# Hybrid streaming encoder step: forget rows spread by DMA, sample values with the probabilities stationary in four column groups, two attention phases one chunk earlier

## The chip, the cores and the metric

One core of one Trainium2 chip runs the kernel. The metric is the time on the device in microseconds (us), the median of several runs. All data are 32-bit floats.

## The reference, cut to what matters

Two layers work on 256 prompt frames and 32 sample frames (288 columns). Each layer is norm, one input projection, two kinds of attention of 8 heads each, output projection, residual, then norm and a squared-ReLU MLP. Phases A (sparse top-k) and B (forgetting) belong to layer 0, C (stick-breaking) and D (chunk band) to layer 1. The sample frames also see 512 cached keys. What the change touches:

```python
# B, forgetting attention; cum is the inclusive sum of log-forget values
logits = einsum('bthd,bshd->bhts', q, k) * scale
logits = logits + swapaxes(cum_q, 1, 2)[..., None] - cum_k   # one row per head, the same for all queries
probs = softmax(where(k_pos <= q_pos, logits, NEG_INF))
out = einsum('bhts,bshd->bthd', probs, v)
# C: the same last step with stick-breaking weights; D: logits + rel_bias, visible band only
```

## The kernel before

**The weight stream.** All weights come in 756 chunks of 128 x 1024 over SP's queue. ACT copies each to `w_high` (L784), DVE subtracts to get `w_low` (L1063), and TensorE multiplies high*high, high*low and low*high (L352 to L354, and L318 to L320 in the output projections), 24 matmuls of 288 columns a chunk.

**Attention beside it.** Each phase has 10 jobs: eight prompt heads (n = 0 to 7, `n < H`) and two sample jobs (n = 8, 9), each of four heads with 32 queries. Phase A runs beside the chunks of B's input projection, B beside the first half of the output projection (`out_half(..., 0, ...)`, 16 chunks), C beside D's input projection, D beside the second layer's first output half. After chunk w every engine does its "window w": the steps that `START[ph][n]` and `jobs_at(ph, w, late)` give. A job's scores come in window START, its turn (transposes of the probabilities) one later, its values two later for prompt jobs, three (C: four) for sample jobs; on ACT and DVE the exponentials (`before`) and `normalize` precede the chunk's work of the next window, and the order inside a window is fixed by hand. After half 0 the second half starts, which waits for the last `mixed_low` of its phase.

**Names.** `logits` adds bias and mask and takes the maximum; `mixed_high` and `mixed_low` (L903, L1272) copy a result of `values` into the projection's operands. `norm_sums` (L434), `rsqrt` (L842, L845) and `prelude` (L1210) normalise pairs of heads: pairs 4 to 7 are the queries, in windows 0 and 1 of B and D, from POOL's `squares` (L1586). `early` does D's first pairs from window 34 of C on. POOL also loads the biases (L1601), adds the mask (`masked`, L1614) and loads the cached keys and values (L1589, L1592). B's forget rows `neg_cum` are added by matmuls of 8 rows (the second pair at L509 and L510, and L490). Sample values are L560 and L562.

Of the kernel before, what the change touches and what calls it, by code (L numbers as in the profile page):

```python
# [14 lines left out]
P = 128  # L15
D = 2048
# [65 lines left out]
WINDOWS = {ph: s[-1] + (5 if ph == "C" else 4) for ph, s in START.items()}  # L82
# [49 lines left out]
def build(nc, ins, outs):  # L132
    with ExitStack() as ctx:
# [49 lines left out]
        neg_cum = sb("neg_cum", [H, TP + L])  # L183
# [23 lines left out]
        def pair_squares(ph, i):  # L207
            return sqs_dq[i % 2] if ph == "D" and i >= 4 else sqs[i % 2]
# [42 lines left out]
        small = proj[0:SMALL, 16, :]  # L251

# [44 lines left out]
        def _(pe):  # L297
# [176 lines left out]
            def scores(ph, n):  # L474
                c = PH[ph]
                if n == 0:

                    pe.wait_ge(sem(ph + "_normed"), (8 + c["nkv"]) // 2)
                    if ph == "A":
                        pe.wait_ge(sem("B_cum_copied"), 1)  # L480
                if n < H:
# [4 lines left out]
                    for (at, keys), queries in zip(HALVES, (q[:, P:TP], q[:, 0:P])):  # L486
                        last = pe.matmul(ps[:, b, at:at + keys], queries, k[:, 0:keys], start=True, stop=ph != "B")  # L487
                        if ph == "B":

                            last = pe.matmul(ps[:, b, at:at + keys], ident[0:H, n:n + 1].to_broadcast([H, P]),  # L490
                                             neg_cum[:, 0:keys], start=False, stop=True)
                else:
                    u = n - H
                    pe.wait_ge(sem(ph + "_s_read"), n)
                    if ph == "A" and n == H:

                        pe.wait_ge(sem("B_rsqrt"), 4)
                    pe.wait_ge(sem(ph + "_k_past"), 16 * (u + 1) if ph != "A" else 16)
                    for j in range(4):
                        h = 4 * u + j  # L500
                        q = q_tiles(ph, h)[:, 0, TP:T]
                        kp, kn = (k_past[ph][:, u, :], u) if ph == "A" else (k_past[ph][:, j, :], h)
                        pairs_ = [(q, kp, k_tile(ph, kn)[:, TP:T])]
                        if ph == "B":
                            pairs_.append((ident[0:H, h:h + 1].to_broadcast([H, TS]), neg_cum[:, TP:TP + PAST],
                                           neg_cum[:, TP + PAST:TP + L]))
                        for m, (lhs, past, new) in enumerate(pairs_):
                            flags = dict(start=m == 0, stop=m == len(pairs_) - 1)
                            pe.matmul(flat[32 * j:32 * j + 32, 2048:2048 + PAST], lhs, past, **flags)  # L509
                            last = pe.matmul(flat[32 * j:32 * j + 32, 2048 + PAST:2048 + L], lhs, new, **flags)  # L510
                last.then_inc(sem(ph + "_scored"), 1)

            def turn_rest(ph, n):

                pe.wait_ge(sem(ph + "_pt_copied"), H + 2 * (n - H) + 1)
                pe.transpose(ps[0:TS, 6, 0:P], probs[n % 2][:, PAST:L], ident[:, :]).then_inc(sem(ph + "_turned"), 1)

            def turn(ph, n):

                pe.wait_ge(sem(ph + "_probs"), n + 1)  # L520
                if n >= 1:
                    pe.wait_ge(sem(ph + "_pt_copied"), n if n <= H else n + (n - H))
# [5 lines left out]
                else:  # L528
                    for b in range(4):
                        last = pe.transpose(ps[:, 6, b * P:b * P + P], p[:, b * P:b * P + P], ident[:, :])  # L530
                    last.then_inc(sem(ph + "_turned"), 1)

            def values(ph, n):
# [5 lines left out]
                else:  # L539
                    pe.wait_ge(sem(ph + "_pt_copied"), n + 1 if n < H else H + 2 * (n - H + 1))  # L540
# [6 lines left out]
                else:  # L547
# [105 lines left out]
            def window_c(w):  # L653
                prelude("C", w)
                for n in jobs_at("C", w, 3, 4):
# [118 lines left out]
        def _(act):  # L774
# [102 lines left out]
            def pt_copy(ph, n):  # L877
                w = pt[n % 2]
                if n >= 2:

                    act.wait_ge(sem(ph + "_mixed"), n - 1)
                if n < H:
                    act.wait_ge(sem(ph + "_turned"), n + 1)
                    act.activation(w[:, 0:384], ps[:, 6, 0:384], ACT.Copy).then_inc(sem(ph + "_pt_copied"), 1)
                else:
                    act.wait_ge(sem(ph + "_turned"), H + 2 * (n - H) + 1)
                    act.activation(w[:, 0:512], ps[:, 6, 0:512], ACT.Copy).then_inc(sem(ph + "_pt_copied"), 1)

            def pt_copy_rest(ph, n):
                act.wait_ge(sem(ph + "_turned"), H + 2 * (n - H) + 2)  # L890
# [947 lines left out]
```

## Time and profile before

| | |
|---|---|
| median of 3 runs | 2680.01 us (2679.99 to 2680.86) |
| the profiled execution | 2679.78 us, of which the span of the profile is 2678.0 us |
| mean granted TensorE clock | 0.986 of full |
| TensorE matmuls busy | 2639.0 us (99%) |
| VectorE / ScalarE / GpSimd busy | 54% / 37% / 6% |

In a timeline a row is start, duration, engine, line, operation, output<-inputs, rows*columns of the stationary operand, and its count; consecutive matmuls overlap, so the cost of one is the distance to the next start. An fp32 matmul leaves two records. In a windows table a row is the stretch and its length, then the busy us and instructions of PE, PEld, DVE, ACT and POOL (of PE alone where only that was asked for), the granted clock, the DMA share and GB/s. A clock of 1.00 is 2.4 GHz, 0.50 is 1.2 GHz.

### The profile page before, as it was taken

What the parts mean: (1) busy time and instruction counts of PE and PEld (TensorE: products, weight loads), DVE (VectorE), ACT (ScalarE), POOL (GpSimd) and SP (SyncE); (2) the same over time, 40 slices, a digit from 0 to 9 for tenths busy, and PEclk for the clock granted to TensorE, in tenths of its full rate; (3) what the DMA queues carried; (4) which work ended last, traced back from release to release, by engine and by line L of the source; (5) the groups of instructions that cost most, each with busy time, mean ns of one, the idle gap of its engine ahead of it and who ended that gap; (6) DMA issues with size and microseconds to landing.
All of it is one profiled execution on the core that took longest, in us unless ns stands there. A gap on an engine that the chain in (4) does not pass through costs nothing.

```text
span 2678.0 us, 47174 instructions
## 1 busy us (share of the span) xinstructions
PE 2639.0 (99%) x19365; PEld 2580.8 (96%) x19365; DVE 1443.2 (54%) x1630; ACT 996.6 (37%) x1233; POOL 173.2 (6%) x162
## 2 busy tenths in 40 slices
PE   7999999999999999999999999999999999999998
PEld 7989987999999999999999999999999999999998
DVE  6577753754455455455654553558544544544543
ACT  4443442433333333333333442434333333333332
POOL 2011110300000000000200001213000000000000
PEclk9999998999999999999999998999999999999999
DMA  5535432445444555554455543534454555554453
GB/s 204 173 131 166 153 125 95 142 166 165 166 167 166 166 167 167 166 167 164 160 200 166 177 152 131 170 138 158 166 166 165 167 166 167 166 168 167 166 179 132
DMA packets 116350, 431.35 MB, mean 161 GB/s; under 512 B 13936, under 2 KB 14272, under 8 KB 113856
## 3 DMA queue, kind: packets, MB, share of 16 engines
q1 hardware_dynamic: 109440, 398.77, 44.8%
q0 software_dynamic: 5664, 29.56, 3.1%
q8 instruction: 152, 2.49, 0.4%
q10 hardware_dynamic: 1056, 0.22, 0.0%
q14 instruction: 38, 0.31, 0.0%
HBM read 418.31 MB, written 10.11 MB: 160 GB/s over the span
## 4 chain that ended last, share of the span: by engine, by line
PE 96%; DVE 1%; issue 1%; ACT 1%; DMA 0%; SPq 0%; POOL 0%; DVEq 0%; ACTq 0%; POOLq 0%
PE ps L352 27%; PE ps L354 27%; PE ps L353 27%; PE ps L318 3%; PE ps L319 3%; PE ps L320 3%; PE ps L560 1%; PE ps L434 1%; PE ps L509 1%; PE ps L545 1%; PE ps L487 1%; DVE w_low L1063 0%; ACT w_high L784 0%; PE ps L722 0%; PE ps L562 0%
## 5 line engine op out<-in xcount | busy, mean ns | idle before, releaser
L1063 DVE TENSOR_TENSOR w_low<-raw,w_high 128x1024 fp32r<-128x1024 f32 x756 | 952.4, 1260 | 962.7 <-ACT w_high L784 960.1
L784 ACT CAST w_high<-raw 128x1024 fp32r<-128x1024 f32 x756 | 793.3, 1049 | 1472.8 <-PE ps L354 1359.5
L352 PE MATMUL ps<-x_parts,w_high 128*128 128x288 f32 x3472 | 1041.0, 300 | 18.5 <-DVE x_parts L1132 14.5
L353 PE MATMUL ps<-x_parts,w_high 128*128 128x288 f32 x3472 | 1025.1, 295 | 0.0
L354 PE MATMUL ps<-x_parts,w_low 128*128 128x288 f32 x3472 | 1023.4, 295 | 0.0
L352 PEld LDWEIGHTS ps<-x_parts,w_high 128*128 128x128 f32 x3472 | 653.8, 188 | 25.0 <-issue 16.0
L353 PEld LDWEIGHTS ps<-x_parts,w_high 128*128 128x128 f32 x3472 | 659.0, 190 | 3.0 <-issue 2.4
L354 PEld LDWEIGHTS ps<-x_parts,w_low 128*128 128x128 f32 x3472 | 657.9, 189 | 0.0
L352 PE MATMUL ps<-hid_parts_a,w_high 128*128 128x288 f32 x1024 | 303.1, 296 | 0.0
L354 PE MATMUL ps<-hid_high_b,w_low 128*128 128x288 f32 x1024 | 302.3, 295 | 0.0
L353 PE MATMUL ps<-hid_low_b,w_high 128*128 128x288 f32 x1024 | 302.3, 295 | 0.0
L352 PE MATMUL ps<-hid_high_b,w_high 128*128 128x288 f32 x1024 | 301.5, 294 | 0.0
L353 PE MATMUL ps<-hid_parts_a,w_high 128*128 128x288 f32 x1024 | 301.2, 294 | 0.0
L354 PE MATMUL ps<-hid_parts_a,w_low 128*128 128x288 f32 x1024 | 300.8, 294 | 0.0
L353 PEld LDWEIGHTS ps<-hid_parts_a,w_high 128*128 128x128 f32 x1024 | 193.5, 189 | 0.0
L352 PEld LDWEIGHTS ps<-hid_parts_a,w_high 128*128 128x128 f32 x1024 | 191.9, 187 | 1.5 <-DVE w_low L1063 1.5
L354 PEld LDWEIGHTS ps<-hid_parts_a,w_low 128*128 128x128 f32 x1024 | 193.3, 189 | 0.0
L353 PEld LDWEIGHTS ps<-hid_low_b,w_high 128*128 128x128 f32 x1024 | 192.4, 188 | 0.0
L354 PEld LDWEIGHTS ps<-hid_high_b,w_low 128*128 128x128 f32 x1024 | 192.3, 188 | 0.0
L352 PEld LDWEIGHTS ps<-hid_high_b,w_high 128*128 128x128 f32 x1024 | 192.1, 188 | 0.0
L318 PE MATMUL ps<-hid_parts_a,w_high 128*128 128x288 f32 x256 | 82.0, 320 | 0.7 <-DVE hid_parts_a L1272 0.7
L318 PE MATMUL ps<-hid_high_b,w_high 128*128 128x288 f32 x256 | 79.4, 310 | 1.4 <-DVE hid_low_b L1272 1.4
(316 smaller groups left out, 1986.5 us busy)
## 6 DMA issues: line engine op xcount, KB each, us to landing
raw<-in_w SPq DMA_DIRECT2D x756, 512.0 KB, 3.3
resid<-in_x SPq DMA_DIRECT2D x4, 576.0 KB, 7.4
out_y<-resid POOLq DMA_DIRECT2D x8, 288.0 KB, 2.4
scr<-in_k_past_B POOLq DMA_DIRECT2D x2, 1024.0 KB, 5.2
scr<-in_v_past_B POOLq DMA_DIRECT2D x2, 1024.0 KB, 6.1
scr<-in_k_past_C POOLq DMA_DIRECT2D x2, 1024.0 KB, 6.7
scr<-in_v_past_C POOLq DMA_DIRECT2D x2, 1024.0 KB, 8.4
scr<-in_k_past_D POOLq DMA_DIRECT2D x2, 1024.0 KB, 5.9
```

The costliest lines, as they stand in the source:

```text
L318: pe.matmul(out, wh, high, start=k % 8 == 0, stop=False)
L319: pe.matmul(out, wh, low, start=False, stop=False)
L320: last = pe.matmul(out, w_low[:, c % 2, at:at + P], high, start=False, stop=k % 8 == 7)
L352: pe.matmul(out, wh, high, start=k == 0, stop=end and apart)
L353: pe.matmul(out_low, wh, low, start=k == 0 and apart, stop=False)
L354: last = pe.matmul(out_low, w_low[:, kk % 2, at:at + rows], high, start=False, stop=end)
L434: last = pe.matmul(ps[:, b + u, 0:T], ones[:, :], pair_squares(ph, i)[:, u, :], start=True, stop=True)
L487: last = pe.matmul(ps[:, b, at:at + keys], queries, k[:, 0:keys], start=True, stop=ph != "B")
L509: pe.matmul(flat[32 * j:32 * j + 32, 2048:2048 + PAST], lhs, past, **flags)
L545: pe.matmul(ps[:, 7, 0:TP], v[:, 0, :], w[:, 0:TP], start=True, stop=False)
L784: act.copy(w_high[:, kk % 2, :], raw[:, kk, :]).then_inc(high_ready, 1)
L1063: dve.tensor_tensor(w_low[:, kk % 2, :], raw[:, kk, :], w_high[:, kk % 2, :].bitcast(F32), ALU.subtract)\
```

## The change

Four things are edited. (1) `neg_cum` is written once to a DRAM tensor `cum_rows`, and for each B job a DMA spreads its row over the partitions of `addend`; POOL adds the mask and DVE takes `addend` in place of the mask, so that the 8-row matmuls go. (2) Sample values of B, C and D use the probabilities (128 x 32) as stationary and the values (128 columns) as moving operand, each head in its own group of 32 output partitions; ACT copies the rows out (`copy_rows`, in B and D with the division by the sum) and one transpose (`turn_mixed`) a window later brings them back. (3) Jobs of B and D start one window earlier, the last job of A too, and C's sample outputs come one window later. (4) The transposes of a sample job are in one window, and POOL orders bias, mask and squares anew (`addends_beside`).

```diff
 START = {
-    "A": [23 + n for n in range(H)] + [43, 46],
-    "B": [2 + n for n in range(H)] + [10, 12],
+    "A": [23 + n for n in range(H)] + [43, 45],
+    "B": [1 + n for n in range(H)] + [9, 11],
     "C": [1 + 3 * n for n in range(H)] + [25, 29],
-    "D": [2 + n for n in range(H)] + [10, 12],
+    "D": [1 + n for n in range(H)] + [9, 11],
 }
...
-WINDOWS = {ph: s[-1] + (5 if ph == "C" else 4) for ph, s in START.items()}
+WINDOWS = {ph: s[-1] + (6 if ph == "C" else 3 if ph == "A" else 4) for ph, s in START.items()}
...
-        neg_cum = sb("neg_cum", [H, TP + L])
+        neg_cum = sb("neg_cum", [H, WIDE + L])
+        cum_rows = nc.dram_tensor("cum_rows", (H, WIDE + L), F32).ap()
...
-            return sqs_dq[i % 2] if ph == "D" and i >= 4 else sqs[i % 2]
+            return sqs_dq[i % 2] if ph in "BD" and i >= 4 else sqs[i % 2]
...
+        def rows_out(ph, n):
+
+            return (xs if ph == "C" else probs)[n % 2][:, 0:HD]
+
+        def mixed_at(ph, n):
+
+            return ps[:, 7, P:2 * P] if n >= H and ph != "A" else ps[:, 7, 0:P]
...
+                if n == 0 and ph == "A":
+                    pe.wait_ge(sem("A_normed"), (8 + c["nkv"]) // 2)
+                    pe.wait_ge(sem("B_cum_copied"), 1)
+                if ph in "BD" and n < H:
+                    pe.wait_ge(sem(ph + "_normed"), 4 + n // 2 + 1)
+                    if n == 0:
+                        pe.wait_ge(sem(ph + "_ln"), 7)
+                    if n == 1:
+                        pe.wait_ge(sem(ph + "_ln"), 8)
...
-                        last = pe.matmul(ps[:, b, at:at + keys], queries, k[:, 0:keys], start=True, stop=ph != "B")
-                        if ph == "B":
-
-                            last = pe.matmul(ps[:, b, at:at + keys], ident[0:H, n:n + 1].to_broadcast([H, P]),
-                                             neg_cum[:, 0:keys], start=False, stop=True)
+                        last = pe.matmul(ps[:, b, at:at + keys], queries, k[:, 0:keys], start=True, stop=True)
...
+                    if u:
+                        pe.wait_ge(sem(ph + "_pt_copied"), n)
...
-                        pairs_ = [(q, kp, k_tile(ph, kn)[:, TP:T])]
-                        if ph == "B":
-                            pairs_.append((ident[0:H, h:h + 1].to_broadcast([H, TS]), neg_cum[:, TP:TP + PAST],
-                                           neg_cum[:, TP + PAST:TP + L]))
-                        for m, (lhs, past, new) in enumerate(pairs_):
-                            flags = dict(start=m == 0, stop=m == len(pairs_) - 1)
-                            pe.matmul(flat[32 * j:32 * j + 32, 2048:2048 + PAST], lhs, past, **flags)
-                            last = pe.matmul(flat[32 * j:32 * j + 32, 2048 + PAST:2048 + L], lhs, new, **flags)
+                        pe.matmul(flat[32 * j:32 * j + 32, 2048:2048 + PAST], q, kp, start=True, stop=True)
+                        last = pe.matmul(flat[32 * j:32 * j + 32, 2048 + PAST:2048 + L], q, k_tile(ph, kn)[:, TP:T],
+                                         start=True, stop=True)
...
-            def turn_rest(ph, n):
-
-                pe.wait_ge(sem(ph + "_pt_copied"), H + 2 * (n - H) + 1)
-                pe.transpose(ps[0:TS, 6, 0:P], probs[n % 2][:, PAST:L], ident[:, :]).then_inc(sem(ph + "_turned"), 1)
...
-                pe.wait_ge(sem(ph + "_probs"), n + 1)
+                pe.wait_ge(sem(ph + ("_probs" if n < H or ph == "A" else "_exps")), n + 1)
...
-                        last = pe.transpose(ps[:, 6, b * P:b * P + P], p[:, b * P:b * P + P], ident[:, :])
-                    last.then_inc(sem(ph + "_turned"), 1)
+                        pe.transpose(ps[:, 6, b * P:b * P + P], p[:, b * P:b * P + P], ident[:, :])
+                    pe.transpose(ps[0:TS, 5, 384:512], p[:, PAST:L], ident[:, :]).then_inc(sem(ph + "_turned"), 1)
...
+                        for b in range(4):
+                            for j in range(4):
+                                at = b * P + TS * j
+                                pe.matmul(ps[TS * j:TS * j + TS, 7, 0:HD], w[:, at:at + TS], v_past[ph][:, b, j, :],
+                                          start=b == 0, stop=False)
                         for j in range(4):
-                            out = ps[:, 7, TS * j:TS * j + TS]
-                            for b in range(4):
-                                pe.matmul(out, v_past[ph][:, b, j, :], w[:, b * P + TS * j:b * P + TS * j + TS],
-                                          start=b == 0, stop=False)
-                            last = pe.matmul(out, v_new[ph][0:TS, 2, 4 * u + j, :],
-                                             w[0:TS, PAST + TS * j:PAST + TS * j + TS], start=False, stop=True)
+                            at = PAST + TS * j
+                            last = pe.matmul(ps[TS * j:TS * j + TS, 7, 0:HD], w[0:TS, at:at + TS],
+                                             v_new[ph][0:TS, 2, 4 * u + j, :], start=False, stop=True)
...
+            def turn_mixed(ph, n):
+
+                pe.wait_ge(sem(ph + "_rows_copied"), n - H + 1)
+                pe.transpose(mixed_at(ph, n), rows_out(ph, n), ident[:, :]).then_inc(sem(ph + "_rows_turned"), 1)
...
-                for n in jobs_at(ph, w, 2, 3):
+                for n in jobs_at(ph, w, 3):
+                    if n >= H and ph in "BD":
+                        turn_mixed(ph, n)
+                for n in jobs_at(ph, w, 2):
                     values(ph, n)
...
-                for n in jobs_at(ph, w, 2):
-                    if n >= H:
-                        turn_rest(ph, n)
...
+                for n in jobs_at("C", w, 5):
+                    if n >= H:
+                        turn_mixed("C", n)
...
+                act.wait_ge(sem(ph + "_mixed"), n + 1)
+                if ph == "C":
+                    act.activation(rows_out(ph, n), ps[:, 7, 0:HD], ACT.Copy).then_inc(sem(ph + "_rows_copied"), 1)
+                else:
+                    act.wait_ge(sem(ph + "_inv"), n - H + 1)
+                    act.activation(rows_out(ph, n), ps[:, 7, 0:HD], ACT.Copy, scale=inv[:, n % 2, 0:1])\
+                       .then_inc(sem(ph + "_rows_copied"), 1)
...
+                for n in jobs_at("C", w, 3, 5):
                     mixed_high("C", n)
+                for n in jobs_at("C", w, 4):
+                    if n >= H:
+                        copy_rows("C", n)
...
+                if n < 2 and ph in "BD":
+                    dve.wait_ge(sem(ph + "_normed"), 7 + n)
                 if ph == "B":
-                    if n == 0:
-                        dve.wait_ge(sem("B_masks"), 32)
+                    dve.wait_ge(sem("B_addend"), n + 1)
...
-                                mask_b[:, at:at + keys], ALU.add, ALU.add)
+                                addend[n % 2][:, at:at + keys], ALU.add, ALU.add)
...
+                if n >= H and ph in "BD":
+                    dve.reciprocal(inv[:, r, 0:1], total[:, r, 0:1]).then_inc(sem(ph + "_inv"), 1)
+                    return
...
+                landed_ = sem(f"{ph}_bias{n % 2}")
+                if ph == "B":
+
+                    pool.wait_ge(sem("B_rows"), 16)
+                    if n < H:
+                        pool.dma_start(addend[n % 2][:, 0:WIDE], cum_rows[n:n + 1, 0:WIDE].to_broadcast([P, WIDE]))\
+                            .then_inc(landed_, 16)
+                    else:
+                        for j in range(4):
+                            h = 4 * (n - H) + j
+                            pool.dma_start(addend[n % 2][TS * j:TS * j + TS, 0:L],
+                                           cum_rows[h:h + 1, WIDE:WIDE + L].to_broadcast([TS, L])).then_inc(landed_, 16)
+                    return
...
+                elif ph == "B":
+                    if n == 0:
+                        pool.wait_ge(sem("B_masks"), 32)
+                    m = mask_b if n < H else mask_bs
...
+                    if n == 0:
+                        pool.wait_ge(sem("D_mask"), 16)
...
+            def addends_beside(ph):
+
+                for n in range(2):
+                    masked(ph, n)
+                squares(ph, 4, 8)
+                for n in range(2, JOBS):
+                    bias(ph, n)
+                    if n - 1 >= 2 and (n - 1 < H or ph == "B"):
+                        masked(ph, n - 1)
+                if ph == "B":
+                    masked(ph, JOBS - 1)
...
+            pool.wait_ge(sem("B_cum_copied"), 1)
+            pool.dma_start(cum_rows[:, :], neg_cum[:, :]).then_inc(sem("B_rows"), 16)
...
-            squares("B", 4, 6)
+            bias("B", 0)
+            bias("B", 1)
             pool.wait_ge(hid_low_ready, hid_at["B"])
             load_quad("B", 0)
             load_quad_v("B", 0)
-            squares("B", 6, 8)
+            addends_beside("B")
             second_quad("B")
...
-            squares("D", 4, 8)
-            pool.wait_ge(sem("D_mask"), 16)
-            addends("D", 0, JOBS)
+            bias("D", 0)
+            bias("D", 1)
+            addends_beside("D")
```

## Rows read from the trace of the kernel before

**Rows 1.** The page: busy time by engine, and the chain that ended last, by engine.
```profile
PE 2639.0 (99%) x19365; PEld 2580.8 (96%) x19365; DVE 1443.2 (54%) x1630; ACT 996.6 (37%) x1233; POOL 173.2 (6%) x162
...
PE 96%; DVE 1%; issue 1%; ACT 1%; DMA 0%; SPq 0%; POOL 0%; DVEq 0%; ACTq 0%; POOLq 0%
```

**Rows 2.** Windows table: chunks alone; first of seven half-clock stretches, their sum.
```profile
560.00:700.00 140.00, 140.00 (x1060) 140.00 (x1059) 70.47 (x68) 50.25 (x50) 0.00 (x0) 1.00 0.50 166
...
345.71:355.84 10.13, 9.08 (x36) 8.27 (x36) 0.63 (x2) 0.55 (x2) 1.12 (x2) 0.50 0.58 208
...
sum 60.19, PE 58.14 PEld 55.95 DVE 4.53 ACT 5.18 POOL 5.59; mean PE 8.31 PEld 7.99 DVE 0.65 ACT 0.74 POOL 0.80
```

**Rows 3.** Windows table of TensorE alone: six single jobs, start to end.
```profile
415.93:424.20 8.27, 8.27 (x33) 1.00 0.19 65
1765.57:1766.64 1.07, 1.07 (x17) 1.00 0.10 32
366.06:368.04 1.98, 1.98 (x11) 1.00 0.13 52
1725.38:1726.01 0.63, 0.63 (x6) 1.00 0.47 189
336.92:338.31 1.39, 1.39 (x12) 1.00 0.65 165
1794.08:1799.41 5.33, 5.33 (x42) 1.00 0.57 189
```

**Rows 4.** Timeline of TensorE: sample scores of B (one head), then D's.
```profile
415.93 1.05 PE L509 MATMUL ps<-scr,proj 128*32 128x512 f32 x2
...
416.97 1.04 PE L509 MATMUL ps<-neg_cum,ident 8*32 8x512 f32 x2
...
1765.57 1.08 PE L509 MATMUL ps<-scr,proj 128*32 128x512 f32 x8
```

**Rows 5.** Timeline of TensorE: tail of A and its last waits, then B's.
```profile
344.31 0.66 PE L530 MATMUL ps<-ident,tmp 128*128 128x128 f32 x4 [1.47 <-DVE tmp L1259]
345.71 0.40 PE L516 MATMUL ps<-ident,tmp 128*32 128x128 f32 x1 [0.75 <-ACT scr L887]
...
349.96 0.61 PE L318 MATMUL ps<-hid_parts_a,w_high 128*128 128x288 f32 x1 [0.69 <-DVE hid_parts_a L1272]
...
466.88 0.61 PE L318 MATMUL ps<-hid_high_b,w_high 128*128 128x288 f32 x1 [0.69 <-DVE hid_low_b L1272]
```

**Rows 6.** Timeline of DVE and POOL around A's end.
```profile
342.14 2.11 DVE L1259 TENSOR_SCALAR tmp<-tmp,inv 128x544 f32<-128x544 f32 x1
...
341.69 2.26 POOL L1586 TENSOR_TENSOR acc<-proj 128x576 f32<-128x576 f32 x2
350.20 0.58 POOL L1589 DMA_DIRECT2D scr<-in_k_past_B  x1 [6.26 <-DVE hid_parts_a L1272]
```

**Rows 7.** Timeline of ACT, DVE, POOL: C's last window but one, and D's first loads.
```profile
1652.92 1.04 ACT L784 CAST w_high<-raw 128x1024 fp32r<-128x1024 f32 x1 [1.76 <-PE ps L354]
...
1654.00 1.23 DVE L1063 TENSOR_TENSOR w_low<-raw,w_high 128x1024 fp32r<-128x1024 f32 x1 [2.51 <-ACT w_high L784]
1659.64 0.29 DVE L1272 TENSOR_TENSOR hid_parts_a<-ps,hid_parts_a 128x128 fp32r<-128x128 f32 x1 [4.41 <-ACT hid_parts_a L903]
...
1660.22 0.55 POOL L1690 DMA_DIRECT2D scr<-in_mask_d  x1 [32.96 <-DVE hid_parts_a L1272]
```

**Rows 8.** Timeline of DVE and TensorE: D's last query pair, first logits, first turn.
```profile
1724.32 0.96 DVE L1210 SCALAR_TENSOR_TENSOR proj<-proj,qk_gain,tmp 128x576 f32<-128x576 f32 x1 [0.53 <-ACT tmp L845]
...
1727.86 0.55 DVE L1236 TENSOR_TENSOR tmp<-ps,acc 128x384 f32<-128x384 f32 x1
...
1730.92 0.33 PE L525 MATMUL ps<-ident,tmp 128*128 128x128 f32 x1 [1.50 <-DVE tmp L1256]
```

**Rows 9.** The page: DMA issues, KB each, median us from issue to landing.
```profile
scr<-in_k_past_B POOLq DMA_DIRECT2D x2, 1024.0 KB, 5.2
...
acc<-in_bias_A POOLq DMA_DIRECT2D x8, 192.0 KB, 3.5
```

More of the change, by code:

```diff
@@ L902, in mixed_high, with copy_rows @@
                     f = f0 + 4 * (n - H)
-                    act.activation(hid(True, f, 4)[:, :, TP:T], ps[:, 7, 0:P].rearrange("p (j t) -> p j t", j=4),
+                    act.activation(hid(True, f, 4)[:, :, TP:T], mixed_at(ph, n).rearrange("p (j t) -> p j t", j=4),
                                    ACT.Copy).then_inc(hid_high_ready, 1)
+            def copy_rows(ph, n):
+                act.wait_ge(sem(ph + "_mixed"), n + 1)
+                if ph == "C":
[4 more added lines that the diff above has]
+                       .then_inc(sem(ph + "_rows_copied"), 1)
             def attend(ph, w):
+                for n in jobs_at(ph, w, 3):
+                    if n >= H and ph in "BD":
+                        mixed_high(ph, n)
                 for n in jobs_at(ph, w, 1):
@@ L909, in attend @@
                 for n in jobs_at(ph, w, 2):
-                    if n >= H:
-                        pt_copy_rest(ph, n)
-                for n in jobs_at(ph, w, 2, 3):
-                    mixed_high(ph, n)
+                    if n >= H and ph in "BD":
+                        copy_rows(ph, n)
+                    else:
+                        mixed_high(ph, n)
             def dots_relu(x):
@@ L1225, in logits @@
                                 p[:, at:at + keys], ps[:, 4 + n % 2, at:at + keys], cum_q[:, 1 - i, n:n + 1],
[L1226 removed]
+                                addend[n % 2][:, at:at + keys], ALU.add, ALU.add)
                     else:
                         last = dve.scalar_tensor_tensor(p[:, 0:L], flat[:, 2048:2048 + L],
[L1229 removed]
+                                                        cum_qs[:, n - H:n - H + 1], addend[n % 2][:, 0:L],
+                                                        ALU.add, ALU.add)
                 else:
@@ L1252, in normalize @@
                 m = 2 if n < H else 1
+                if n >= H and ph in "BD":
+                    dve.reciprocal(inv[:, r, 0:1], total[:, r, 0:1]).then_inc(sem(ph + "_inv"), 1)
+                    return
                 link(dve.reciprocal(inv[:, r, 0:m], total[:, r, 0:m]))
@@ L1277, in attend @@
                     logits(ph, n)
-                for n in jobs_at(ph, w, 2, 3):
+                for n in jobs_at(ph, w, 2, 3 if ph in "BD" else 2):
                     mixed_low(ph, n)
@@ L1462, in window_c @@
                     scale_q()
-                for n in jobs_at("C", w, 3, 4):
+                for n in jobs_at("C", w, 3, 5):
                     mixed_low("C", n)
@@ L1598, in bias @@
                     pool.wait_ge(sem(ph + "_s_read"), n - 1)
+                landed_ = sem(f"{ph}_bias{n % 2}")
[4 more added lines that the diff above has]
+                            .then_inc(landed_, 16)
+                    else:
+                        for j in range(4):
[3 more added lines that the diff above has]
+                    return
                 a, rows = (addend[n % 2][:, 0:WIDE], ins["bias_" + ph][n]) if n < H else \
                     (addend[n % 2][:, 0:L], ins[f"bias_{ph}_s"][n - H])
-                pool.dma_start(a, rows).then_inc(sem(f"{ph}_bias{n % 2}"), 16)
+                pool.dma_start(a, rows).then_inc(landed_, 16)
             def masked(ph, n):
-                pool.wait_ge(sem(f"{ph}_bias{n % 2}"), 16 * (n // 2 + 1))
+                pool.wait_ge(sem(f"{ph}_bias{n % 2}"), 16 * (n // 2 + 1) + (48 if ph == "B" and n >= H else 0))
                 a = addend[n % 2][:, 0:WIDE] if n < H else addend[n % 2][:, 0:L]
```

29 lines of the change are left out of this document (11 added, 18 removed).

## The prediction

> **What bounds the kernel.** I read the page first: TensorE has matmuls in flight 99% of the time, and the chain that ended last runs through it for 96% [rows 1]. So the time is TensorE's work, and the question is what each of its jobs costs from start to start, not how long a record is. Next the windows table, for the clock. A chunk is 24 x 140 / 1060 = 3.17 us at full clock, 3.3 behind fp32 matmuls [rows 2]. In seven stretches of together 60.19 us the granted clock is at half, 1.2 GHz; TensorE is busy in 58.14 us of them [rows 2]. One opens in the waits at A's tail, two in or behind sample values of B, two of C, two of D; ahead of six of them TensorE ran small matmuls of 32 moving columns. Then single jobs in the timeline [rows 3, 4], and last the ends and beginnings of phases, where TensorE does wait [rows 5 to 8].
>
> **Forget rows.** A sample job's scores in B take 8.27 us, in D, where there are no forget rows, 1.07 us, although the rows themselves are only half of B's matmuls [rows 3]. The timeline says why: D issues the matmuls of its four heads, each in its own 32 output partitions, as one group of 8 records in 1.08 us; B's first head alone takes 1.04 us from its start to that of its 8-row matmul [rows 4]. The alternation of 128-row and 8-row operands keeps the four groups apart. Without it B's job should be D's: 2 x (8.27 - 1.07) = 14.4 us. A prompt job's scores: 1.98 us against D's 0.63, 8 x 1.35 = 10.8 us. Together 25.2 us. On the other side stand DMAs that I price at nothing: a row spread over 128 partitions is 192 KB, as A's bias, which lands in 3.5 us [rows 9]; jobs follow each other by (1765.57 - 1725.38) / 8 = 5.0 us in D [rows 3] and each buffer has two of these. DVE's sum has as many inputs as before, and POOL's ten mask additions lie beside chunks.
>
> **Sample values.** One job at full clock takes 5.33 us for 20 matmuls [rows 3]. The new job has as many, of 128 moving columns. The nearest row for that shape is A's: five in 1.39 us [rows 3], four in a column of 128 cached keys and one of 32 rows. The change gives each of four heads exactly five, in four column groups. If the groups run side by side as D's scores do, the job costs about 1.4 us; if they don't, 4 x 1.39 = 5.6. I take 1.4, because D's four heads cost what B's one does. Six jobs: 6 x (5.33 - 1.4) = 23.6 us. The six added transposes come at some 0.2 us each (bounds 0.1 and 0.4; four in a row take 0.66 us to the end of the last [rows 5]), 1.2 us back: 22.4 us. ACT's row copies are hidden by a whole chunk, as the transpose comes one window later.
>
> The Trainium skill (TensorE: Matmul & The Clock Gate, Part 3, what overlaps and what doesn't) says that a weight load overlaps with matmuls in flight only when its row group differs. In the new job all cached keys fill all rows and each matmul has its own weights, so by that rule the groups would queue and the job would be nearer 5.6 us. D's scores, which also load weights in between, ran side by side in 1.07 us, so the trace speaks against it; the row has long matmuls, though, and these are short.
>
> **The clock.** The low stretches begin with the jobs that become short, so I take them all as gone: half of 58.14 is 29.1 us. That includes C's second sample job, whose 32-column scores stand right behind the values and ran at half speed. The bounds are no gain at all, if each fall finds another cause, and all 29.1.
>
> **Ends of phases.** A's last job moves from window 46 to 45, so its values no longer lie behind the last chunk with nothing beside. In place of waits of 1.47, 0.75 and 0.69 us [rows 5], I expect 0.2 at the turn (DVE's multiplication took 2.11 us while POOL squared [rows 6]; the squares now come later) and 1.3 before the output half: behind the last chunk ACT's cast, DVE's subtraction and then `mixed_low` stand in line, 2.7 us after the chunk, against 1.4 of values. Saved: 2.91 - 1.5 = 1.4 us. At the ends of B and D the last job is complete a window before half 1, so 0.69 us each is saved [rows 5], D as B. Together 2.8 us.
>
> **New waits.** They come from the earlier start and from a faster TensorE.
> - B, window 0: `squares` 4 and 5 were done by 344 [rows 6]. Now they stand behind two key and value loads (released 0.25 us after the half begins, 1.1 us) and two mask additions (each 1.1, as the squares' 1.13), and squares 4 itself takes 1.13: ready after 4.7 us, while TensorE arrives after one chunk, 3.3 us. Wait 1.4, and 0.35 for the second: 1.75 us.
> - First job of D: the scores come right behind the last `norm_sums` and wait 0.25 us for ACT's read of the bank. The logits must wait for both query pairs, 1724.32 + 0.96 = 1725.28. From logits to turn the chain is 1730.92 - 1727.86 = 3.06 us [rows 8], so the turn is at 1728.4, while TensorE, which before came to its first scores at 1725.38 [rows 3], arrives there plus 0.63 and 0.25, at 1726.2: 2.2 us. That is 2.45 against 1.50 before: 0.95 us. In B the same 2.45 against a wait of 0.27 before: 2.2 us.
> - From C to D: `early` D still begins in window 34, and `turn_mixed` of C's last job is now in that window too. Its copy waits on ACT behind the cast, its `mixed_low` on DVE behind the subtraction: in window 33 the cast begins at 1652.92, an estimated 0.25 us behind its chunk, and the subtraction ends at 1655.23 [rows 7], so 2.6 us after the chunk, then 0.29. POOL follows 0.29 later [rows 7], issues three DMAs (1.63 us) and squares (1.13): 5.9 us, of which 0.3 is the transpose. Wait 5.6 us. Before, values and a chunk at half speed covered all of it. Such a gap is longer than those at A's tail behind which the clock fell, so I add a half-clock stretch of some 6 us, 3.0 us.
> - Second key loads of B wait for POOL's last mask addition. Between the two sample jobs lie two chunks and their jobs, some 8 us, and a load needs 0.6 + 5.2 [rows 6, 9]. I take nothing, up to 2 us.
>
> Together 1.75 + 0.95 + 2.2 + 5.6 + 3.0 = 13.5 us.
>
> **The sum.** - 25.2 - 22.4 - 29.1 - 2.8 + 13.5 = - 66.0 us. The profiled execution took 2679.78 us, 1.78 more than its span and 0.2 under the median, so both give 2613.8, I say 2614 us.
>
> **Rivals.**
> - The column groups queue (chance 0.09; the skill's rule above): 6 x 4.2 = 25 us less gain, 2639 us. For it: 32-wide weights are loaded 40 times a job. Against: D's scores.
> - The clock falls elsewhere (0.16): at the waits at B's and D's start, and at C's second sample scores, which keep their 32-column matmuls. Three stretches of the common 6.8 us give 10 us back, 2624 us. For it: TensorE is idle 2 us at a time there. Against: before D's 1.50 us no fall followed.
> - The gap from C to D is short, or the clock stands it (0.10): up to 8.6 us better, 2605 us.
> - Slower than before (0.02): the spread rows land late, since 128 partitions read one DRAM row. Two job periods less POOL's and DVE's part, some 7 us, are free; beyond that each job waits half the excess, and with ten jobs a landing of 20 us would eat all 66. A's bias needs 3.5, so this needs nearly six times as much.
> - No effect within 0.2% (0.01): only if several of these fall together.
> - My forecast (0.62): 2608 to 2620 us.
>
> The likeliest is 2614. The range reaches down to the short gap and a share of the tails, 2603, and up past the clock's rival, with B's key load late, 2630; the queueing groups are left out. A change of 0.2% is what a measurement here tells from none; faster 0.97, same 0.01, slower 0.02.
>
> **What would show it.** B's sample scores as 8 records in about 1.1 us; sample values at about 1.4 us and no row of 32 moving columns in them; full clock through B and D; a TensorE wait for `squares` of 5 to 6 us at the start of D's early pairs, and half clock behind it; waits of about 2 us at the first turns of B and D. I am wrong if the values' records stand one behind another, or if TensorE waits for logits in every window of B, which would be the DMA.

## The result, and the profile after

The changed kernel takes 2621.26 us (median; 2619.10 to 2621.31 over four runs) against 2680.44 beside it: ratio 0.9769, 95% interval 0.9756 to 0.9782. The forecast was 2614. The profiled executions are 58.6 us apart (2679.78 and 2621.22), of 66.0 forecast; the forecast's own span of 2608 to 2620 was missed by 1 us, the range of 2603 to 2630 holds the time.

The page after, busy time by engine and the chain by engine, beside [rows 1]:

```profile
PE 2570.9 (98%) x19307; PEld 2527.5 (97%) x19307; DVE 1441.1 (55%) x1627; ACT 998.3 (38%) x1239; POOL 193.6 (7%) x189
...
PE 95%; DVE 2%; issue 1%; ACT 1%; POOL 1%; DMA 0%; SPq 0%; DVEq 0%; ACTq 0%; POOLq 0%
```

Single jobs in the windows table of TensorE (columns as in [rows 3]): B's sample scores, B's prompt scores, sample values of B, then of C.

```profile
401.87:402.94 1.07, 1.07 (x17) 1.00 0.00 0
384.57:385.15 0.58, 0.58 (x7) 1.00 0.15 58
410.69:412.05 1.36, 1.36 (x41) 1.00 0.66 256
1581.39:1582.75 1.36, 1.36 (x41) 1.00 0.00 0
```

B's scores fell from 8.27 to 1.07 us and from 1.98 to 0.58 [rows 3], and the values from 5.33 to 1.36: the three durations on which most of the sum rests came out within 0.05 us.

The windows table of the clock, from the end of A's sample work to the last chunk, has two stretches at half clock where [rows 2] had seven. Ahead of the first stands what led into it.

```profile
1557.91:1560.80 2.89, 2.89 (x29) 1.00 0.20 60
1560.80:1567.60 6.80, 6.80 (x35) 0.50 0.59 204
1612.00:1618.80 6.80, 4.92 (x16) 0.50 0.94 341
```

The second begins in the gap between C and D, as forecast. The first begins 2.9 us into C's first sample scores (L733, 32 moving columns), where the kernel before kept its full clock; this one was not forecast.

The list of TensorE's waits (total, times, longest), start-up waits left out:

```profile
PE ps L526 <- DVE tmp L1286: 7.1, 5, 1.8
PE ps L443 <- POOL acc L1617: 5.6, 1, 5.6
...
PE ps L327 <- DVE hid_parts_a L1302: 1.3, 1, 1.3
PE ps L443 <- POOL scr L1617: 1.0, 1, 1.0
```

The gap between C and D is 5.62 us (forecast 5.6), A's tail 1.35 (1.5), B's wait for squares 1.04 (1.75). The turns (L526) waited 1.82 us in B's first window and 1.64 in D's, and twice more late in B, 1.29 and 1.00, which no step foresaw. The timeline of DVE and POOL shows those two places:

```profile
391.91 2.01 POOL L1640 DMA_DIRECT2D acc<-cum_rows  x4 [3.51 <-DVE tmp L1250]
...
393.52 1.58 DVE L1285 TENSOR_SCALAR tmp<-tmp,inv 128x256 f32<-128x256 f32 x1
393.93 1.01 POOL L1664 TENSOR_TENSOR acc<-acc,scr 128x384 f32<-128x384 f32 x1
...
397.63 1.99 POOL L1640 DMA_DIRECT2D acc<-cum_rows  x4 [2.69 <-DVE tmp L1250]
...
399.24 1.90 DVE L1285 TENSOR_SCALAR tmp<-tmp,inv 128x256 f32<-128x256 f32 x1
399.63 1.35 POOL L1664 TENSOR_TENSOR acc<-acc,scr 128x544 f32<-128x544 f32 x1
```

DVE's scaling of the exponentials has a median of 0.353 us over 24 instances, as the view of its line says:

```profile
L1285 DVE TENSOR_SCALAR tmp<-tmp,inv x24: 352/353/1899, 241.7 to 1713.8; 128x256 f32<-128x256 f32 x24
```

In these two places it takes 1.58 and 1.90 and ends just behind POOL's mask addition. The addition is late because the four DMAs of a sample job take POOL 2.0 us to issue. In the four windows of B before them one issue of 0.57 us stands there, and the addition ends as the scaling begins (387.37 + 1.02 against 388.39).

Last, the end of the program, the last two rows of the timeline of before and of after:

```profile
2668.86 0.76 DVE L1124 TENSOR_TENSOR resid<-resid,ps 128x576 f32<-128x576 f32 x1 [4.01 <-PE ps L354]
2669.91 0.54 POOL L1704 DMA_DIRECT2D out_y<-resid  x1 [12.18 <-DVE resid L1124]
```

```profile
2608.65 0.75 DVE L1149 TENSOR_TENSOR resid<-resid,ps 128x576 f32<-128x576 f32 x1 [4.01 <-PE ps L363]
2609.70 0.54 POOL L1769 DMA_DIRECT2D out_y<-resid  x1 [12.17 <-DVE resid L1149]
```

From the last issue to the end of the span it is 8.1 us before (2678.0 - 2669.91) and 9.5 after (2619.2 - 2609.70): 1.4 us lost behind all work.

### The profile page after: what moved, and what is told of

Read it like the earlier page. It is cut to its first block, busy times and chain, and to the rows that moved or that the text cites. A ratio compares the mean times of both kernels' runs of the same rounds, so it can differ in the third digit from the quotient of the medians.

```text
span 2619.2 us, 47119 instructions
## 1 busy us (share of the span) xinstructions
PE 2570.9 (98%) x19307; PEld 2527.5 (97%) x19307; DVE 1441.1 (55%) x1627; ACT 998.3 (38%) x1239; POOL 193.6 (7%) x189
## 4 chain that ended last, share of the span: by engine, by line
PE 95%; DVE 2%; issue 1%; ACT 1%; POOL 1%; DMA 0%; SPq 0%; DVEq 0%; ACTq 0%; POOLq 0%
PE ps L361 28%; PE ps L363 27%; PE ps L362 27%; PE ps L327 2%; PE ps L329 2%; PE ps L328 2%; PE ps L443 1%; DVE w_low L1088 1%; ACT w_high L795 1%; PE ps L546 0%; PE ps L500 0%; PE ps L733 0%; PE ps L601 0%; DVE x_parts L1157 0%; DMA resid<-in_x 0%
## 5 line engine op out<-in xcount | busy, mean ns | idle before, releaser
L361 PE MATMUL ps<-hid_high_b,w_high 128*128 128x288 f32 x1024 | 301.3, 294 | 0.0
L1149 DVE TENSOR_TENSOR resid<-resid,ps 128x576 f32<-128x576 f32 x64 | 48.3, 754 | 55.9 <-PE ps L363 55.9
```

Source lines behind the costliest of these rows:

```text
L361: pe.matmul(out, wh, high, start=k == 0, stop=end and apart)
L1149: dve.tensor_tensor(r, r, ps[:, 2 * odd:2 * odd + 2, 0:T], ALU.add).then_inc(evacuated, 1)
```

## Experiments

Each is an edit of the changed kernel unless said otherwise, and the code cuts are abridged. The runs came in three sets, each beside the kernel before on its chip: 2679.6 us there for experiments 1 to 4, 2683.7 for 5 to 7 and the first of 8, 2681.1 for the rest. Ratios are to that. Differences in us are to the changed kernel's 2621.26 us, and between sets they carry a few us of the chips' own.

**1. Do the column groups run side by side?** The order of the sample values' loops:

```diff
-for b in range(4):
-    for j in range(4):
-        pe.matmul(ps[TS*j:TS*j+TS, 7, 0:HD], w[:, at:at+TS], v_past[ph][:, b, j, :], ...)
+for j in range(4):
+    for b in range(4):
+        pe.matmul(ps[TS*j:TS*j+TS, 7, 0:HD], w[:, at:at+TS], v_past[ph][:, b, j, :], ...)
```

> The changed kernel (2621 us) with the sample values' loops exchanged: the head outside, the block of cached keys inside, so that five matmuls in a row go to one group of 32 output partitions. Same 20 matmuls, same operands. Theory 1, groups run side by side only when neighbouring matmuls go to different groups: a job goes from 1.36 us to 4 x 1.39 = 5.6 us, 6 x 4.2 = 25 us more, about 2646 us, and up to 10 us more if the clock falls behind the longer jobs. Theory 2, a matmul with 32 stationary columns is cheap in any order: the job stays at 1.4 us, 2621 us.

2644.83 us, ratio 0.9869 (0.9853 to 0.9886), 23.6 us more. One job in the windows table, then its first two heads in the timeline:

```profile
411.73:417.01 5.28, 5.28 (x41) 1.00 0.40 144
```

```profile
411.73 1.06 PE L561 MATMUL ps<-scr 128*32 128x128 f32 x8
412.72 0.40 PE L564 MATMUL ps<-scr 32*32 32x128 f32 x2
413.05 1.06 PE L561 MATMUL ps<-scr 128*32 128x128 f32 x8
```

Each head costs 1.32 us and the four queue: 5.28 against 1.36, 3.9 times, with the same matmuls. Six jobs make 6 x 3.92 = 23.5 us. Theory 1 holds: it is the order, and not the narrow stationary operand. One thing changed beside it. The changed kernel's timeline has the same job in two rows:

```profile
410.69 1.08 PE L561 MATMUL ps<-scr 128*32 128x128 f32 x32
411.70 0.42 PE L565 MATMUL ps<-scr 32*32 32x128 f32 x8
```

By head, the 32-row matmul of each head stands between matmuls of 128 rows, and experiment 3 shows that alternating heights keep groups apart too. But the four 128-row matmuls of one head alone, all of one height, take 0.99 us (411.73 to 412.72), and all sixteen of the job take 1.01 in the changed kernel (410.69 to 411.70). So most of the loss is the queue inside a group; what the height adds between the heads was not tried apart.

**2. Was it the old shape that lowered the clock?** Only the operands of the sample values are exchanged back:

```diff
-pe.matmul(ps[TS*j:TS*j+TS, 7, 0:HD], w[:, at:at+TS], v_past[ph][:, b, j, :], ...)   # and so the fifth
+pe.matmul(ps[:, 7, TS*j:TS*j+TS], v_past[ph][:, b, j, :], w[:, at:at+TS], ...)      # heads outside
```

> The changed kernel with only the operands of the sample values' matmuls exchanged back (values stationary, 32 columns of probabilities moving), into the same 128 x 128 of PSUM; copies and the added transpose stay, so sample outputs are wrong. A job goes from 1.36 to 5.33 us: 6 x 3.97 = 23.8 us. Theory 1, the clock fell before because of these matmuls: half-clock stretches come back behind most of the six jobs, 3 to 5 of 6.8 us, 10 to 17 us more: 2655 to 2662 us. Theory 2, the clock fell for B's 8-row scores and the waits at A's tail, or for C's own scores: no new stretch in B and D, 2645 us.

2663.41 us, ratio 0.9933 (0.9915 to 0.9950), 42.1 us more than the changed kernel. Half clock is back in B, C and D; the windows table of two of its stretches:

```profile
414.50:421.30 6.80, 6.80 (x38) 0.50 0.43 131
1595.50:1612.60 17.10, 17.10 (x81) 0.50 0.26 93
```

Its seven stretches last 57.9 us, against 13.6 in the changed kernel. 23.8 us of matmuls and half of the other 44.3 us make 46, and with the price of half clock worked out further down they make 42.3; the measured 42.1 is far from theory 2's 24. The clock gain hangs on the values' operands, and not on the length of the jobs: those of experiment 1 last 5.28 us, and its profile has no low stretch in B or D. No stretch stands at A's tail, so the one there went with A's earlier last job or the shorter waits; which of the two was not tried apart.

**3. What made B's sample scores 8.27 us?** The kernel before, with only this order changed:

```diff
-for j in range(4):
-    for m, (lhs, past, new) in enumerate(pairs_):   # query matmuls, then 8-row matmuls
+for m in range(2):                                  # query matmuls of all heads first
+    for j in range(4):
+        lhs, past, new = by_head[j][m]
```

> The kernel before (2680 us) with B's sample scores reordered: first the query matmuls of the four heads, then their four 8-row matmuls, same operands and count. Theory 1, the alternation of 128-row and 8-row operands keeps the column groups apart: a job goes from 8.27 to 2 x 1.07 = 2.1 us, 12.3 us less, 2668 us (a few us less still if a half-clock stretch of B goes with it). Theory 2, 8-row matmuls queue among themselves: 1.07 + 4 x 1.04 = 5.2 us a job, 2674 us. Theory 3, the order does nothing: 2680 us.

2667.71 us, ratio 0.9957 (0.9941 to 0.9972), 11.9 us less than before. The two jobs in the windows table:

```profile
417.91:420.06 2.15, 2.15 (x34) 1.00 0.03 8
427.81:429.96 2.15, 2.15 (x34) 1.00 0.42 164
```

Each job takes 2.15 us, twice 1.07, in place of 8.27: 12.2 us in two jobs, theory 1. So the forecast's reading of [rows 4] was right, and 12 of its 14.4 us were to be had without a DMA. The Trainium skill has the rule for it (TensorEngine Tiling (Array Packing), Tiling Modes, Key Properties): tiles run in parallel, but a change of tiling mode drains the engine. The alternation of 128-row and 8-row operands fits it, 8.27 against 2.15 us. The same section of the Trainium skill lets tiles of one mode load weights and multiply in parallel. The changed kernel agrees (1.36 us with 20 weight tiles), and speaks against the other rule of the Trainium skill (TensorE: Matmul & The Clock Gate, Part 3) that the forecast weighed.

**4. What is the earlier start worth?** 

```diff
-    "B": [1 + n for n in range(H)] + [9, 11],   # D alike
+    "B": [2 + n for n in range(H)] + [10, 12],
```

> The changed kernel with the jobs of B and D started at chunk 2, 10 and 12 again. Theory 1, the early start bought two end waits of 0.69 us with longer waits at the first turns (1.82 us in B, 1.64 in D): B loses 1.55 us of wait and gets 0.69 back, D 0.14 and 0.69, so the time stays within 1 us of 2621. Theory 2, the earlier start is worth what it saves at the end and more: 2 to 3 us slower. Theory 3, it costs time: the late waits of B (1.29 and 1.00 us) go too and it is 3 us faster.

2627.82 us, ratio 0.9806 (0.9790 to 0.9822), 6.6 us more. Its list of waits:

```profile
PE ps L526 <- DVE tmp L1286: 7.2, 5, 1.7
PE ps L443 <- POOL acc L1617: 5.6, 1, 5.6
PE ps L327 <- DVE hid_low_b L1302: 5.1, 2, 2.5
```

Theory 2 had the direction, but none of the three the mechanism. The turns wait as long as with the earlier start (1.74 us in B's first one, 1.55 in D's). B's wait came from the short scores and not from the start: 0.27 us before, and the scores are 1.40 us shorter. D's was there before, 1.50. And the ends of B and D now wait 2.54 us each, because the new transposition of the last sample job stands behind the last chunk; in B a half-clock stretch of 3.4 us follows. 5.1 us and what the half clock costs, about 1.4, are the loss. The earlier start makes room for the added step.

**5. The gap between C and D.** One number, D's early pairs one chunk later:

```diff
-W_EARLY = {"B": 33, "D": 34}
+W_EARLY = {"B": 33, "D": 35}
```

> The changed kernel (2621 us) with D's early key pairs started in window 35 of C instead of 34 (one number), one chunk behind the last transposition of C. Theory 1, the 5.62 us wait and the half clock behind it come from both lying in one window: the wait falls to 5.62 minus a chunk of 3.3, or to 2.3 us, and the 6.8 us half-clock stretch behind it goes (2.5 us): about 5.8 us less, 2615.5 us. Theory 2, the clock falls behind C's second sample scores whatever the wait does: only the 3.3 us, 2618 us. Theory 3, the later pairs are late for D's first chunk of the output projection: no gain.

2613.69 us (2612.34 to 2619.54), ratio 0.9739 (0.9723 to 0.9755), 7.6 us less than the changed kernel's median. The wait is 2.46 us and TensorE keeps its clock behind it, as the windows table shows; ahead of it, in the same execution, the clock fell behind both of C's sample scores:

```profile
1562.20:1569.00 6.80, 6.80 (x35) 0.50 0.62 219
1586.10:1592.90 6.80, 6.80 (x36) 0.50 0.53 213
1612.00:1625.00 13.00, 10.54 (x73) 1.00 0.75 268
```

The profiled execution is the slowest of the five (2619.54), by about the two stretches: its mean granted clock is 0.994, that of the other four 0.996 to 0.997. All eight profiles whose wait is 5.6 us have half clock behind it; the four with 2.46 or 0.60 us have none.

**6. The late turns of B.**

```diff
 for n in range(2, JOBS):
-    bias(ph, n)
-    masked(ph, n - 1)
+    masked(ph, n - 1)
+    bias(ph, n)                 # in B; D keeps its order
```

> The changed kernel with POOL's order in B turned round: first the mask addition of job n - 1, then the DMAs that spread the rows of job n. In the changed kernel the additions of jobs 7 and 8 stand behind four DMA issues each (2.0 us) and so fall on DVE's scaling of the exponentials, which then takes 1.58 and 1.90 us instead of 0.35; TensorE waits 1.29 and 1.00 us at the turn. Theory 1, the two operations meet on the engines' way to memory: without the meeting both waits go, 2.3 us less, 2619 us. Theory 2, the scaling is slow for another reason (its data, a semaphore): the waits stay, 2621 us.

2618.65 us (2614.73 to 2619.82), ratio 0.9755 (0.9738 to 0.9771). The medians differ by 2.6 us, but the interval overlaps that of the changed kernel (0.9756 to 0.9782), so the trace has to decide. In the timeline the scalings at both places, and the addition that now comes ahead of the issues:

```profile
388.50 1.66 POOL L1664 TENSOR_TENSOR acc<-acc,scr 128x384 f32<-128x384 f32 x1 [2.85 <-DMA acc<-cum_rows]
390.23 2.06 POOL L1640 DMA_DIRECT2D acc<-cum_rows  x4
```

```profile
391.84 0.35 DVE L1285 TENSOR_SCALAR tmp<-tmp,inv 128x256 f32<-128x256 f32 x1
...
396.68 0.35 DVE L1285 TENSOR_SCALAR tmp<-tmp,inv 128x256 f32<-128x256 f32 x1
```

Both are back at 0.35 us and both waits are gone; the four issues beside a scaling cost it nothing, the addition did. The Trainium skill states it (SBUF — State Buffer, Who interferes with whom): `tensor_scalar` in its two-port mode and a GpSimd operation want the same port pair, and the second blocks until the first has ended. The trace agrees on the length: DVE's 399.24 to 401.14 ends behind POOL's 400.98. It differs on who should win: DVE's row begins 0.4 us ahead of POOL's, and yet DVE is the one that waits. At its usual 0.35 us it would even have ended before POOL's row begins (393.52 + 0.35 against 393.93), so the two rows don't show the whole of what each holds. That stays open.

The gain is seen without the other executions' noise in layer 0's output projection, from its first matmul to the first one behind it: 134.45 to 134.55 us in the five profiles with nothing changed in B, 132.07 to 132.18 in the three with the masks alone changed there (this one and the two of experiment 9). That is 2.4 us, with a spread of 0.1.

**7. Both edits, and B's squares 4 and 5 ahead of the loads.**

```diff
+squares("B", 4, 6)
 load_quad("B", 0)
 load_quad_v("B", 0)
 addends_beside("B")             # in it squares 6 and 7 stay, behind masked(0) and masked(1)
```

> The changed kernel with both of the edits above, and with POOL's squares 4 and 5 of B ahead of the two loads of cached keys and values. If each wait is separate: 5.8 us from the gap between C and D, 2.3 us from the late turns, 1.04 us from the wait for squares in B's window 0: 9.1 us less, 2612 us. Rival: the loads of keys and values now leave 2.3 us later and the half clock moves on to another place: 2615 to 2618 us.

2612.57 us (2611.67 to 2613.48), ratio 0.9734 (0.9718 to 0.9749). The wait for squares is gone, but the next ones take its place: 1.93 us at the first turn with half clock behind it, and 0.49 at the third.

```profile
363.10:366.50 3.40, 3.40 (x15) 0.50 0.36 102
```

Layer 0's output projection takes 132.9 us here (346.38 to 479.29) and 132.1 with the masks alone (344.74 to 476.81): the squares' edit lost 0.8 in this one profile, with the half clock in it.

**8. C's 32-column scores and the clock.** Three of four heads left out:

```diff
-for j in range(4):              # past scores of a sample job of C
+for j in range(1):
```

> The changed kernel with only the first head's 32-column score matmuls of C's two sample jobs; those of the other three heads are left out, so the sample outputs of C and what follows are wrong. The matmuls left out cost 2 x 3/4 x 3.5 = 5.3 us at full clock. Theory 1, these matmuls make the clock fall at 1560.8 us of the changed kernel: no half-clock stretch there, 3.4 us more gained, 2612 to 2613 us. Theory 2, the fall has another cause in C: it stays, 2616 us.

2610.63 us, ratio 0.9727 (0.9709 to 0.9745), 10.6 us less, and 2612.05 in the profiled execution. There is no half clock in C but in the gap, in one profile: theory 1. (5.3 us of matmuls left out and 3.4 of clock were expected, 8.7.) Then the changed kernel again, and the scores split with nothing left out:

```diff
+for n in jobs_at("C", w + 1):          # one window ahead, sample jobs: heads 0 and 1
+    if n >= H:
+        past_sticks(n, 0, 2)
...
-    for j in range(4): ...             # 16 matmuls of 32 moving columns
+    past_sticks(n, 2, 4)               # heads 2 and 3 where all four were
```

> The changed kernel once more, unchanged, beside the next three on the same chip. Theory 1, the half-clock stretch in C at 1560.8 us and the one in the gap between C and D belong to the kernel: both are there again within a few us of their place, 2621 us. Theory 2, where the clock falls behind C's sample scores is decided anew in each execution: the first stretch stands behind the second sample scores (near 1585 us), or behind both or neither, and single runs differ by about 3.4 us.

> The changed kernel with the 32-column score matmuls of C's two sample jobs split: two heads one chunk earlier, two heads where they were, the same matmuls in all. Theory 1, the clock falls because 3.5 us of such matmuls stand in one piece: in halves of 1.8 us with a chunk between them there is no fall in C ahead of the gap, 3.4 us less, 2618 us, and the runs lie closer together. Theory 2, their number counts and not their place: 2621 us, the fall is there a little earlier or later.

The unchanged kernel: 2622.88 us (2619.80 to 2623.04), ratio 0.9777 (0.9764 to 0.9791); this time the clock fell behind both scores and in the gap:

```profile
1559.70:1566.50 6.80, 6.80 (x35) 0.50 0.58 218
1583.60:1590.40 6.80, 6.80 (x36) 0.50 0.53 218
1614.30:1621.10 6.80, 5.59 (x19) 0.50 0.96 346
```

The split one: 2616.99 us (2616.31 to 2618.95), ratio 0.9760 (0.9746 to 0.9773), full clock through C up to the gap:

```profile
1556.00:1609.90 53.90, 49.92 (x424) 1.00 0.42 141
1610.00:1616.80 6.80, 5.27 (x18) 0.50 0.91 330
```

All eight profiles with the new values and the scores in one piece have half clock behind the first scores (two), the second (four) or both (two). The three with the scores cut or split have none. That each execution decides anew where it falls is the second theory of the repeated run, and it holds; experiment 5's runs, all on one chip, differ in the same way. That the clock falls behind the first scores is new with the changed kernel, four profiles of eight against none of three with the old values; why was not tried.

**9. Together.** Experiments 5 and 6 with D's first square ahead of three DMAs, and then the split scores too.

```diff
+squares("D", 0, 1)
 pool.dma_start(mask_d, ...)
 load_quad("D", 0)
 load_quad_v("D", 0)
-squares("D", 0, 4)
+squares("D", 1, 4)
```

> The changed kernel with D's early pairs from window 35 and B's mask additions ahead of its DMAs (as tried before), and POOL's first square of D ahead of the mask's and the two loads' DMAs. The wait behind C was 2.46 us with the window alone; the three issues ahead of the square took 1.63 us: 0.8 us of wait left. Sum against the changed kernel: -5.8 (window) - 2.4 (masks) - 1.6 = 9.8 us less, 2611 to 2612 us. Rival: the square's place gives nothing, because POOL's later squares come late instead, 2613 us.

> The kernel of squares_d_first with C's split sample scores as well. If the edits add up: 3.4 us less than that kernel, about 2608 us, and no half-clock stretch between 220 us and the last chunk. Rival: the clock falls anyway in C, 2611 us.

2610.95 us (2608.39 to 2614.19), ratio 0.9738 (0.9724 to 0.9751), the gap at 0.60 us; and 2608.18 us (2606.80 to 2610.08), ratio 0.9729 (0.9715 to 0.9742), with full clock from A's sample work to the last chunk. The intervals of the two overlap; what splitting does for the clock is read from the profiles.

```profile
220.00:2590.00 2370.00, 2358.33 (x17814) 1.00 0.51 167
```

This last kernel is 14.7 us ahead of the changed one in the same set, 0.6%, with nothing left out.

## Why the prediction was right, and by how much it was off

| term | forecast | measured |
|---|---|---|
| forget rows | 14.4 + 10.8 | 2 x (8.27 - 1.07) = 14.4; 8 x (1.98 - 0.58) = 11.2 |
| sample values, transposes | 23.6 - 1.2 | 6 x (5.33 - 1.36) = 23.8; 0.1 each, 0.6 |
| half clock gone | 29.1 | 29.1 - 3.4 (half of 6.80, C's sample scores) = 25.7; repriced below |
| ends of phases | 1.4 + 1.4 | 2.91 - 1.35 = 1.6; 1.4 |
| B, squares | -1.75 | -1.04 |
| first turns of B and D | -2.2 - 0.95 | -(1.82 - 0.27) - (1.64 - 1.50) = -1.7 |
| from C to D | -5.6 - 3.0 | -5.62 - 2.5 (half of 4.92) = -8.1 |
| late turns of B | 0 | -2.3 |
| behind the last issue | 0 | -1.4 |
| sum | 66.0 | 62.9 by these rows, 58.6 between the profiled executions |

The mechanism was right in the large terms, but for a part of the clock's. **Forget rows**: the reading of the timeline was right, and experiment 3 shows it apart from the DMAs, which landed in 3.5 us as priced. **Sample values**: D's scores were the right row to price them from; experiment 1 shows what the rival of queueing groups would have cost, 23.6 us of its 25. **From C to D**: wait and half clock as worked out.

**The step that failed** is the clock's, "so I take them all as gone", which included C's second sample job. The values' operands did carry the low clock (experiment 2), but C's own 32-column scores suffice to lower it somewhere: 6.8 us in the profile of the changed kernel, behind the first scores, and 13.6 us in its second profile, behind both (experiment 8). The rival "the clock falls elsewhere" named the second scores and came true in one of its three places: the waits at B's and D's starts lowered nothing in the changed kernel. The misses have both signs; the squares and the first turns came out 2.2 us better than forecast.

**The step that was left out** is in the forget rows, "POOL's ten mask additions lie beside chunks". They lie beside chunks and also beside DVE, and two of ten fall on a scaling that lasts until they end. The forecast had the row for it, DVE's 2.11 us while POOL squared [rows 6], used it for A's tail, and did not ask it of the ten additions that the change moves to POOL.

**Mis-sized**: the waits at first turns were costed against the earlier start, 3.15 us, and came to 1.7; in B the wait belongs to the shortened scores (experiment 4), and in D it came to 1.64 us and not 2.45. The squares' wait was 0.7 us shorter. The end of the program, 1.4 us, was not looked at: all twelve profiles of kernels that spread the rows by DMA have 10.5 us behind the last matmul, the kernel before and the regrouped one, which don't, 9.2. The whole of it is one instruction, POOL's closing drain, 6.59 us against 5.21. POOL issues 80 DMAs in the changed kernel and 63 before; whether these or the added DRAM tensor lengthen the drain was not tried.

The clock's term was priced too high as well. The forecast and the table take half of each low stretch, as if half the clock took twice the time. The timeline of the changed kernel has the starts of a chunk's matmuls on both sides of the end of a stretch:

```profile
1616.44 0.44 PE L363 MATMUL ps<-x_parts,w_low 128*128 128x288 f32 x1
1616.68 0.44 PE L361 MATMUL ps<-x_parts,w_high 128*128 128x288 f32 x1
...
1619.10 0.29 PE L363 MATMUL ps<-x_parts,w_low 128*128 128x288 f32 x1
1619.23 0.29 PE L361 MATMUL ps<-x_parts,w_high 128*128 128x288 f32 x1
```

They follow each other in 0.24 us at half clock and in 0.13 at full (median 0.132), 1.8 times; 32-column ones in 0.213 and 0.112, 1.9 times. With the medians of each kind of matmul at both clocks, and nothing for time in which TensorE waits, the seven stretches of the kernel before cost an estimated 26.8 us and the two of the changed kernel 5.4: a gain of 21.4 us where the table has 23.2. That is 1.8 of the 4.3 us between the table's sum and the measured time. The other 2.5 us are left open; among them are tenths in many windows, such as turns that wait 0.1 to 0.2 us below what the list of waits shows.

## What to carry to other kernels

Small matmuls that can take a group of 32 output partitions each ran side by side here only where neighbours in the program went to different groups and had operands of the same height, so look at the order of the loops before looking at the operands: 5.28 against 1.36 us, 8.27 against 2.15. When TensorE gets faster, price every step beside it again, above all what another engine moves next to a DVE operation that slows down beside it (0.35 us became 1.90), and what stands alone behind the last chunk of a phase. A run of 32-column matmuls cost twice here, in its own time and in the half clock behind it; cut in two with a chunk between, it cost only the first. And half clock is not twice the time: measure one matmul at either clock before pricing a stretch.

## What the hardware showed that was not expected

The place where the clock falls is not fixed by the program: two profiles of the same kernel have it behind the first of C's sample scores, and behind both. Single runs of the kernel before lay between 2673.4 and 2689.4 us in the first two sets, with mean granted clocks of 0.990 and 0.982, and those of the last kernel within 3.3 us. A wait of TensorE of 5.6 us had half clock behind it in eight of eight profiles, one of 2.46 us in none of two.

DVE's `tensor_scalar` of 128 x 256 took 0.35 us in the median and up to 1.90 beside an addition of POOL; four DMA issues of POOL beside it cost nothing. DVE's subtraction, whose mean is 1.26 us, was slow beside an addition that had begun before it:

```profile
401.50 1.35 POOL L1664 TENSOR_TENSOR acc<-acc,scr 128x544 f32<-128x544 f32 x1 [0.52 <-DMA acc<-cum_rows]
401.92 2.02 DVE L1088 TENSOR_TENSOR w_low<-raw,w_high 128x1024 fp32r<-128x1024 f32 x1
```

In experiment 6 an addition that began behind a subtraction took 1.66 us in place of 1.02 (the row at 388.50). And a 128-partition spread of one row of DRAM, 192 KB, landed in 3.5 us, as fast as a load of 192 KB from 128 rows.
